# Building the relative-bias table in the first mixer's opening, and loading expert weights in 16 KB pieces

## The reference

```python
def clamped_swiglu(hgu):
    gate, up = jnp.split(hgu, 2, axis=-1)
    gate = jnp.minimum(gate, SWIGLU_LIMIT)
    up = jnp.clip(up, -SWIGLU_LIMIT, SWIGLU_LIMIT)
    return gate * jax.nn.sigmoid(SWIGLU_ALPHA * gate) * (up + 1)
...
        return clamped_swiglu(xb @ w1[e] + b1[e]) @ w2[e] + b2[e]
```

```python
        bias = rel_bias[t5_bucket(sel - tq[None, :, None])]
        logits = logits + jnp.moveaxis(bias, -1, 2).astype(jnp.float32)
```

## Time and profile before

| | |
|---|---|
| median of 3 runs | 2480.67 us (2477.57 to 2481.11) |
| the profiled execution, its own time | 2479.01 us |
| its span | 2476.8 us |
| TensorE (matmuls) busy | 2194.0 us, 89% |
| VectorE busy | 841.2 us, 34% |
| ScalarE busy | 352.9 us, 14% |
| transfers | 603.43 MB, mean 244 GB/s |
| granted TensorE clock, mean | 0.96 |

### The profile page before, as it was taken

The page is one execution under the profiler, slowest core; times in us unless marked ns, Lnnn a source line. Parts: engine busy times, 40 slices in busy tenths (PEclk is TensorE's granted clock), DMA queues, the critical chain, the costliest instruction groups (busy, mean ns, idle before and its releaser), DMA issues.

```text
span 2476.8 us, 23637 instructions
## 1 busy us (share of the span) xinstructions
PE 2194.0 (89%) x9258; PEld 1129.7 (46%) x9259; DVE 841.2 (34%) x1276; ACT 352.9 (14%) x740; POOL 44.4 (2%) x25
## 2 busy tenths in 40 slices
PE   4998877899999988999998599988999899898999
PEld 2856632222222222222222264445884554547873
DVE  1454431222222222222221234532561066414650
ACT  1123110000000000000001112211110122202110
POOL 0001100000000000000000001000000010000000
PEclk9998978999999999999999799999999999899999
DMA  9464038999999999999999534223442533133441
GB/s 364 144 244 163 28 78 300 409 410 410 410 410 410 410 410 410 410 410 410 410 410 409 213 135 170 92 94 105 150 156 86 177 132 126 68 102 126 146 158 46
DMA packets 219517, 603.43 MB, mean 244 GB/s; under 512 B 10159, under 2 KB 66495, under 8 KB 219315
## 3 DMA queue, kind: packets, MB, share of 16 engines
q1 hardware_dynamic: 219442, 602.42, 64.6%
HBM read 599.25 MB, written 3.15 MB: 243 GB/s over the span
## 4 chain that ended last, share of the span: by engine, by line
issue 59%; PE 35%; DVE 3%; ACT 1%; DMA 1%; POOL 1%; SPq 0%; DVEq 0%; POOLq 0%
PE bank L560 16%; PE bank L568 7%; PE bank L2002 6%; PE bank L767 2%; PE bank L2233 1%; PE bank L552 1%; DMA ring<-in_w_ada_dram 1%; POOL arena L1518 0%; PE bank L434 0%; PE bank L421 0%; PE bank L1909 0%; DVE hbuf L1647 0%; DVE arena L1648 0%; DVE normw L2118 0%; DVE arena L2090 0%
## 5 line engine op out<-in xcount | busy, mean ns | idle before, releaser
L1193 PE MATMUL bank<-ring,arena 128*64 128x512 f32 x3168 | 719.1, 601 | 103.2 <-DMA ring<-in_w_dram 101.9
L1193 PEld LDWEIGHTS bank<-ring,arena 128*64 128x64 f32 x3168 | 217.7, 138 | 595.4 <-issue 410.4
L560 PE MATMUL bank<-hTbuf,ring 128*128 128x256 f32 x1856 | 401.8, 379 | 4.4 <-ACT hTbuf L1755 3.6
L560 PEld LDWEIGHTS bank<-hTbuf,ring 128*128 128x128 f32 x1856 | 352.4, 190 | 53.0 <-issue 5.5
L2002 PE MATMUL bank<-ring 128*128 128x512 f32 x352 | 151.4, 592 | 0.0
L568 PE MATMUL bank<-ring,hTbuf 128*128 128x512 f32 (+2 forms) x384 | 151.2, 554 | 0.0
L992 DVE COPY arena<-bank 128x256 f32<-128x256 f32 x33 | 14.0, 424 | 370.2 <-PE bank L1187 370.2
L1717 DVE SCALAR_TENSOR_TENSOR arena<-bank,arena 128x254 f32<-128x254 f32 (+1 forms) x176 | 76.6, 477 | 127.7 <-ACT arena L1848 126.1
L1919 PE MATMUL bank<-ring,hTbuf 128*128 128x512 f32 x256 | 115.3, 604 | 0.0
L978 DVE RECIPROCAL arena<-arena 128x512 f32<-128x512 f32 x33 | 110.6, 3353 | 1.1
L568 PEld LDWEIGHTS bank<-ring,hTbuf 128*128 128x128 f32 x384 | 72.7, 190 | 75.1 <-issue 71.8
(11 more groups left out here) (348 smaller groups left out, 1697.5 us busy)
## 6 DMA issues: line engine op xcount, KB each, us to landing
ring<-in_w_dram SPq DMA_DIRECT2D x198, 2048.0 KB, 23.7
ring<-in_w_up_dram SPq DMA_DIRECT2D x44, 1024.0 KB, 6.4
ring<-in_w_in_dram SPq DMA_DIRECT2D x21, 2048.0 KB, 8.3
ring<-in_w_ada_dram SPq DMA_DIRECT2D x12, 2048.0 KB, 8.0
ring<-in_w_down_dram SPq DMA_DIRECT2D x10, 2048.0 KB, 7.8
ring<-in_w_out_dram SPq DMA_DIRECT2D x6, 2048.0 KB, 9.1
ring<-in_w_in_dram SPq DMA_DIRECT2D x4, 1024.0 KB, 14.0
ring<-in_w_proj_a_dram SPq DMA_DIRECT2D x2, 2048.0 KB, 7.9
```

The lines of the kernel that those rows point to most:

```text
L560: ins = pe.matmul(B.bank(name, j)[:, i * T:(i + 1) * T], w[:, k, (first + i) * P:(first + i + 1) * P], hT[:, k, :], start=(k == 0), stop=( ...
L1193: ins = pe.matmul(bank[g * SLOTS:(g + 1) * SLOTS, :], lhsT, rhs[:, g * CH:(g + 1) * CH], start=start, stop=stop)
```

## The change

The bias table's product moves to TensorE's opening, behind the transpose of the convolution's weights; ScalarE instead of VectorE scales it into `relrow`, which now lies at `12 * D + 512`. SyncE writes the row as it is (16 KB) to a new tensor `bias_row` ahead of load 12, and expands it from device memory to device memory behind load 21. The expert chunks are cut differently: chunk 0 to 3 is now a block of 256 rows with gate and up columns, each partition takes two neighbouring rows (16 KB in one piece), and a `w2` chunk gives each partition four neighbouring rows. `up` adds for each chunk to both banks, so that gate and up are both complete with chunk 3. So that the features match these rows, the second modulation deals the features out anew (`dealt`, `held`), the router's weights are loaded in the same order, and the product L988 reads with a step of four.

```diff
-    for name, n in (("ag0", 1), ("ad0", 4), ("hT", 4), ("convT", 1), ("qk", 4), ("dq", 6), ("v", 2), ("z", 2), ("ab", 1),
+    for name, n in (("ag0", 1), ("ad0", 4), ("hT", 4), ("convT", 1), ("rel", 1), ("qk", 4), ("dq", 6), ("v", 2), ("z", 2), ("ab", 1),
...
+        def dealt(row):
+
+            return [row[:, 2 * P * c:2 * P * (c + 1)].rearrange("p (q k) -> p k q", k=2) for c in range(4)]
+
+        def held(row):
+            return [split(row[:, 2 * P * c:2 * P * (c + 1)], 2) for c in range(4)]
...
-                then(v.scalar_tensor_tensor(out=h[:, tt, :], in0=x[:, tt, :], scalar=rs[:, tt:tt + 1], in1=scale,
-                                            op0=ALU.mult, op1=ALU.mult))
+                for hp, xp, sp_ in zip(held(h[:, tt, :]), deal(x[:, tt, :]), deal(scale)):
+                    ins = v.scalar_tensor_tensor(out=hp, in0=xp, scalar=rs[:, tt:tt + 1], in1=sp_, op0=ALU.mult, op1=ALU.mult)
+                then(ins)
...
-            modulate(v, then, 1, 1, ("ad2", 3), 2)
+            modulate(v, then, 1, 1, ("ad2", 3), 2, dealt, held)
...
-            v.wait_ge(*B.ready("rel"))
-            v.tensor_scalar(relrow, B.bank("rel")[0:8, :], float(AHD ** 0.5), None, ALU.mult).then_inc(B.free("rel"), 1)
...
-            v.scalar_tensor_tensor(out=act_b, in0=ub, scalar=1.0, in1=gb_, op0=ALU.add, op1=ALU.mult).then_inc(F["act"], 1)
+            v.scalar_tensor_tensor(out=act_b.rearrange("p (q a) -> p q a", q=4), in0=ub.rearrange("p (a q) -> p q a", q=4),
+                                   scalar=1.0, in1=gb_.rearrange("p (a q) -> p q a", q=4),
+                                   op0=ALU.add, op1=ALU.mult).then_inc(F["act"], 1)
...
-                for ch, (bank, flag) in enumerate(((GB, "gate_h"), (GB, "gate_f"), (UB, "up_h"), (UB, "up_f"))):
+                for ch in range(4):
                     w, landed = wts(i, ch)
                     pe.wait_ge(*landed)
-                    for k in range(4):
-                        ins = halves(bank, xe[:, 4 * (ch % 2) + k, :], w[:, k, :], False, ch % 2 == 1 and k == 3)
-                    ins.then_inc(F[flag], 1)
+                    for m, bank in enumerate((GB, UB)):
+                        for k in range(2):
+                            ins = halves(bank, xe[:, 2 * ch + k, :], w[:, k, m * D:(m + 1) * D], False, ch == 3 and k == 1)
+                        if ch == 3:
+                            ins.then_inc(F[("gate_f", "up_f")[m]], 1)
+                    if ch < 3:
+                        ins.then_inc(F[f"c{ch}"], 1)
...
-            rows = slice((ch % 2) * CH, (ch % 2 + 1) * CH)
             if ch < 4:
-                src = A["w1"][0, e, rows, (ch // 2) * D:(ch // 2 + 1) * D]
-            else:
-                src = A["w2"][0, e, rows, :]
-            return src.rearrange("(k p) n -> p k n", p=P)
+                return A["w1"][0, e, 2 * P * ch:2 * P * (ch + 1), :].rearrange("(p k) n -> p (k n)", p=P)
+            return A["w2"][0, e, CH * (ch - 4):CH * (ch - 3), :].rearrange("(p k) n -> p (k n)", p=P)
...
-            sp.wait_ge(*B.taken("rel"))
-            sp.dma_start(scratch.rearrange("p h n -> h p n"), relrow.unsqueeze(1).to_broadcast([8, P, REL]))\
-              .then_inc(S["rel_out"], 16)
...
-                                       (wrt, A["w_router"][0].rearrange("(k p) n -> p k n", p=P)),
+                                       (wrt.rearrange("p (c k) n -> p c (k n)", c=4),
+                                        A["w_router"][0].rearrange("(c p k) n -> p c (k n)", c=4, p=P)),
...
+                if n == ada_at[1]:
+
+                    sp.wait_ge(*B.taken("rel"))
+                    sp.dma_start(row8, relrow).then_inc(S["rel_row"], 16)
...
+            sp.wait_ge(S["rel_row"], 16)
+            sp.dma_start(scratch.rearrange("p h n -> p (h n)"), row8.rearrange("h n -> (h n)").partition_broadcast(P))\
+              .then_inc(S["rel_out"], 16)
...
+            act.wait_ge(*B.ready("rel"))
+            act.activation(relrow, B.bank("rel")[0:8, :], ACT.Copy, scale=float(AHD ** 0.5)).then_inc(B.free("rel"), 1)
...
+            pe.wait_ge(*B.room("rel"))
+            pe.matmul(B.bank("rel")[0:8, :], thin[0:32, 0:8], c("bucket", 32), start=True, stop=True)\
+              .then_inc(B.full("rel"), 1)
```

More of the change, by code:

```diff
@@ L237 @@
     "ov_hot",
-    "rel_out", "rel_in",
+    "rel_row", "rel_out", "rel_in",
     "b12_in", "norm_in",
@@ L246 @@
     "pgt_f", "pgt",
-    "gate_h", "gate_f", "up_h", "up_f", "y_h",
+    "c0", "c1", "c2", "gate_f", "up_f", "y_h",
     "g_in", "gu_out",
@@ L392, in bview, with whole, modulate @@
             return b[:].rearrange("p (a b) -> p a b", a=n)
-        def modulate(v, then, sh, nw, job, count):
+        def dealt(row):
+            return [row[:, 2 * P * c:2 * P * (c + 1)].rearrange("p (q k) -> p k q", k=2) for c in range(4)]
+        def held(row):
+            return [split(row[:, 2 * P * c:2 * P * (c + 1)], 2) for c in range(4)]
+        def whole(row):
+            return [row]
+        def modulate(v, then, sh, nw, job, count, deal=whole, held=whole):
             shift, scale = mod[:, 3 * sh * D:(3 * sh + 1) * D], mod[:, (3 * sh + 1) * D:(3 * sh + 2) * D]
@@ L400, in modulate @@
             for tt in range(TT):
-                then(v.scalar_tensor_tensor(out=h[:, tt, :], in0=x[:, tt, :], scalar=rs[:, tt:tt + 1], in1=scale,
-                                            op0=ALU.mult, op1=ALU.mult))
+                for hp, xp, sp_ in zip(held(h[:, tt, :]), deal(x[:, tt, :]), deal(scale)):
+                    ins = v.scalar_tensor_tensor(out=hp, in0=xp, scalar=rs[:, tt:tt + 1], in1=sp_, op0=ALU.mult, op1=ALU.mult)
+                then(ins)
             for tt in range(TT):
-                v.tensor_tensor(h[:, tt, :], h[:, tt, :], shift, ALU.add).then_inc(S["h_new"], 1)
+                for hp, sp_ in zip(held(h[:, tt, :]), deal(shift)):
+                    ins = v.tensor_tensor(hp, hp, sp_, ALU.add)
+                ins.then_inc(S["h_new"], 1)
         def head(place):
@@ L868, in build_program @@
         r3T = split(area(11 * D, 4 * P), 4)
-        relrow = area(11 * D + 512, REL)[0:8, :]
+        relrow = area(12 * D + 512, REL)[0:8, :]
         xe = split(area(0, CH), KT)
@@ L1140, in moe_t, with view @@
             ins.then_inc(B.full("gT"), 1)
-            pe.wait_ge(*B.room("rel"))
-            pe.matmul(B.bank("rel")[0:8, :], thin[0:32, 0:8], c("bucket", 32), start=True, stop=True)\
-              .then_inc(B.full("rel"), 1)
             wait_all(pe)
-            def view(s):
-                return slot(s).rearrange("p (k n) -> p k n", k=4)
+            def view(s, ch):
+                return split(slot(s), 2 if ch < 4 else 4)
             def weights(i, ch):
@@ L1152, in weights @@
                     s = (N1 + ch) % RING
-                    return view(s), (slot_in[s], 16 * (per_slot[s] + 1))
+                    return view(s, ch), (slot_in[s], 16 * (per_slot[s] + 1))
                 if ch < 4:
                     s = (N1 + 4 + ch) % RING
-                    return view(s), (slot_in[s], 16 * (per_slot[s] + (1 if ch < 2 else 2)) + 16 * (i - 1))
+                    return view(s, ch), (slot_in[s], 16 * (per_slot[s] + (1 if ch < 2 else 2)) + 16 * (i - 1))
                 if isinstance(i, int) and i == NE - 1:
                     s = (N1 + ch) % RING
-                    return view(s), (slot_in[s], 16 * (per_slot[s] + NE))
+                    return view(s, ch), (slot_in[s], 16 * (per_slot[s] + NE))
                 s = (N1 + 4 + ch) % RING
-                return view(s), (slot_in[s], 16 * (per_slot[s] + 2) + 16 * i)
+                return view(s, ch), (slot_in[s], 16 * (per_slot[s] + 2) + 16 * i)
             def over_weights(j, ch):
                 s = (N1 + ch) % RING
-                return view(s), (over_in[s], 16 + 16 * j)
+                return view(s, ch), (over_in[s], 16 + 16 * j)
             def gather(F, n):
@@ L1319, in later_sync @@
                     sp.dma_start(split(biasbuf[:, at:at + 4 * nk], 4), src).then_inc(S["rel_in"], 16)
-            ups, downs = ["gate_h", "gate_f", "up_h", "up_f"], ["y_h", "y_f"]
+            ups, downs = ["c0", "c1", "c2", "up_f"], ["y_h", "y_f"]
             def fetch(s, e, ch, landed):
-                sp.dma_start(slot(s).rearrange("p (k n) -> p k n", k=4), expert_chunk(e, ch)).then_inc(landed[s], 16)
+                sp.dma_start(slot(s), expert_chunk(e, ch)).then_inc(landed[s], 16)
             for ch in (2, 3):
@@ L1342, in later_sync @@
             nov = sp.value_load(ovi[0:1, 15:16], min_val=0, max_val=NOV)
-            before = [("up_h", NE), ("up_f", NE), ("y_h", NE - 1), ("y_f", NE - 1), ("y_h", NE), ("y_f", NE)]
+            before = [("c2", NE), ("up_f", NE), ("y_h", NE - 1), ("y_f", NE - 1), ("y_h", NE), ("y_f", NE)]
             with sp.Fori(0, NOV) as j:
```

5 lines of the change are left out of this document (3 added, 2 removed).

## The result

The changed kernel takes 2421.14 us (median of 4 runs, 2411.08 to 2422.56), beside 2479.12 us (4 runs, 2473.81 to 2481.11) for the kernel before. The ratio is 0.9744, 95% interval 0.9715 to 0.9774: faster by 2.6%. The two medians by themselves are 58.0 us apart, a quotient of 0.9766, which lies in that interval too. The forecast of 2412 is 9.1 us (0.4%) too low; the measured time lies inside its whole range, 2400 to 2453, and just above the narrower 2404 to 2421. The profiled execution is the fastest of the four: 2411.08 us around a span of 2409.2, where the sum gave 2412.2.

A forecast was written before the change was run, and what follows sets the result against it. The expert weight stream was taken as the bound; -71.3 us from earlier start and larger pieces plus 4.5 us took 2479.01 to 2412.2, said as 2412. Its own range was 2404 to 2421, the whole range 2400 to 2453.

The forecast's parts named there:

- What bounds the kernel: Expert stage: weight transfers at 409 to 410 GB/s set the pace; TensorE needs 90.8% of the time.
- the rival in which TensorE becomes the bound: Expert loop: with 1.5 us of slack a round, late chunks cost TensorE time; 2428 us, chance 0.08.
- The wait that goes: SyncE's 43.5 us wait for the bias table's expansion goes; first fetch near 355.1, start alone worth -32.3 us.
- The piece size: Expert chunks in 16 KB instead of 4 KB pieces: 4.91 us a chunk instead of 5.127.
- pieces that stay as dear: Rival: expert stream stays at 410 GB/s, only the earlier start counts; 2451 us, chance 0.14.
- a bad pitch: Rival: 16 KB pieces on a 16 KB pitch stream slower, 5.42 us a chunk; 2503 us, chance 0.07.
- the ceiling of 4.83 us: Rival: no fixed part per piece, 4.83 us a chunk, 14 us less; 2398 us, chance 0.03.
- First landing and last: Expert stream: expert 2's first chunk lands at 388.7, the last awaited at 1267.6 instead of 1338.95, -71.3 us.
- Gate and up by chunk: Both banks complete only with the fourth chunk: hidden in the loop, +4.2 us once in the overflow block.
- The small ones: Opening product +0.6, second modulation +1.0, routing's end -1.9 us: together -0.3 us.
- The sum of 2412.2 us: Whole kernel: -71.3 + 4.5 = -66.8 us from the profiled execution's 2479.01 us.

The follow-up runs named there:

- table-alone kernel: Kernel before with only the bias table moved, expert chunks still in 4 KB pieces: 2447.1 us, ratio 0.9877.
- the kernel with the old form at the new place: Changed kernel with the bias table's expansion again straight from eight partitions in 2 KB pieces, at the new early place: 2419.94 us (one run).
- the 8 KB kernel: Changed kernel with expert chunks in 8 KB pieces, and the plain second modulation and old router weight order: 2427.22 us, ratio 0.978.
- the two repeats: Changed kernel unaltered, measured twice more beside other kernels: 2418.67 us, ratio 0.9744, and 2416.49 us, ratio 0.9741.
- the two with the overflow block by bank: Changed kernel with only the overflow block's up products ordered gate bank first, then up bank, measured twice: 2406.52 us, ratio 0.9731, and 2410.49, ratio 0.9724.

## Why the prediction was right, step by step

**What bounds the kernel.** Held. The weights set the pace to the end of the stage, TensorE waits 34.5 us in 830 us, so it works 95.8% of a round of 29.4 us: 28.1, where the step had 27.9. The margin is 1.2 us and not 1.5, still enough: the rival in which TensorE becomes the bound didn't come. It is near, though; another 4% on the stream would find TensorE there.

**The wait that goes.** Held: no wait, the first fetch at 356.75 (forecast 355.1), no idle at expert 1. The table-alone kernel had its last awaited chunk at 1305.28 against a computed 1306.6. That the expansion has cover was shown by the kernel with the old form at the new place: there it slowed the prefetch by some 20 us, and the closing product was no later.

**The piece size.** Held, and it is the step that decided. Forecast 4.91 us a chunk from a line through 2 KB and 4 KB, which a burst of 13.4 KB bore out; measured 4.90, with the 8 KB kernel on the same line. The rivals that went with it are excluded: pieces that stay as dear would have left 410 GB/s, a bad pitch less, and the ceiling of 4.83 us isn't reached because 9 ns a piece do remain.

**First landing and last.** 1267.6 forecast, 1266.86 measured. That it is so near is partly luck: in the five profiled executions whose program is the same up to this point (this one, the two repeats, the two with the overflow block by bank) it came at 1263.00 to 1268.11.

**Gate and up by chunk.** In the loop hidden, as the step said: there is no wait for VectorE's chain between two experts. In the overflow block the idle is 6.17 us, forecast 5.86 with 0.3 for the strided product beside it: 6.16. That product takes 1.06 us instead of 0.69, both its inputs read in steps of four.

**The small ones.** Of their sum of -0.3 us, -0.07 is left where it counts: expert 1's products begin at 376.19, before at 376.26. But the way there isn't the forecast's. Rows of the changed kernel:

```profile
51.65 1.02 PE L2208 MATMUL bank<-con,small 32*8 32x512 f32 x2
```

```profile
312.49 3.38 DVE L413 SCALAR_TENSOR_TENSOR hbuf<-x,small,arena 128x256 f32<-128x256 f32 x8 [0.67 <-POOL small L2077]
315.91 2.77 DVE L417 TENSOR_TENSOR hbuf<-hbuf,arena 128x256 f32<-128x256 f32 x8
```

```profile
323.33 7.01 PE L1118 MATMUL bank<-arena,hTbuf 128*128 128x32 f32 x32 [0.92 <-ACT hTbuf L557]
```

And the last of them in the kernel before:

```profile
325.79 4.82 PE L1104 MATMUL bank<-arena,hTbuf 128*128 128x32 f32 x32 [0.89 <-ACT hTbuf L543]
```

The opening's extra product took 1.02 us here, and from the transposes (L566) to the first projection it takes 4.68 us, before 4.67: nothing lost. In five of the other nine profiled executions with this product it took 1.87 us, and in three of them, which have this opening unchanged, that stretch is 5.67 to 5.68 us, 1.0 lost. The forecast's 0.6 is the middle of two cases that each occur. The modulation takes 3.38 + 2.77 us instead of 2.60 + 2.36: +1.2, forecast +1.0. It begins 3.7 us earlier than before, at 312.49, for which the sum had no term; in the two repeats it begins at 314.01 and 317.68, so this is the spread of executions and not the change. The router's products then take 7.01 us instead of 4.82, with a granted clock of 0.50 from 324 to 332 us where it was 0.71. The pick begins 0.44 us behind the start of the copy ahead of it instead of 2.30, the -1.9 of the forecast; in time it is 341.17 instead of 343.31. And expert 0's 64 products took 15.96 us instead of 13.95, at 0.87 from 352 to 364 us instead of 1.00. The total came out by terms that cancelled, and that was luck.

**The sum and the median.** The sum of 2412.2 us was for an execution like the profiled one, and such an execution took 2411.08; that the two profiled executions spent the same time in the second block (1078.0 and 1077.9 us) was luck too, as the repeat with 10.2 us more there shows. What was mis-sized is the last step, from there to the median: it set the execution against three runs that lay within 3.5 us and moved it by nothing. Over more runs the kernel before spreads from 2468 to 2491 us, and the changed one from 2409 to 2423. In the one pair of traces taken apart nearly all of it lies in the second block, at a lower granted clock; that it does so in every run isn't shown, nor what sets the clock. A median of four can come out 10 us off for that, as here. The ratio of 0.9744 is 64 us of 2479, with 56 to 71 as its interval, and both the forecast's 66.8 and the medians' 58.0 lie in it. The narrower range of 2404 to 2421 had no term for this spread, and the median, 2421.14, fell just outside.

## What to carry to other kernels

Where a stream of weights sets the pace, fit time per piece against piece size from whatever sizes the trace already has; here the stream's own 4 KB and a short burst of 2 KB gave the pace at 16 KB to 0.2%, and a burst of 13.4 KB bore the line out beforehand. Look in the queue of the engine that issues transfers for one wait that is not for a buffer, and move what it waits for ahead of a long quiet stretch: if it fits in there, its own speed doesn't matter. Compare a forecast with the spread of several executions before calling a small term confirmed. When computation is reordered to suit a transfer, look for the one pass that has no neighbour to hide its tail; it can keep the old order alone.

## What the runs showed of the hardware

- In a stream at a saturated queue, pieces of 4, 8 and 16 KB went at 410, 422 and 428 GB/s. Worked out from these three, each of 16 engines spends 9 ns per piece and 151 ns per 4 KB; an estimate from the slope alone would be 435 GB/s (16 x 4096 B / 150.6 ns).
- 2 MB written to device memory from eight partitions, in 2 KB pieces, went at some 49 GB/s and took 44 us; the same 2 MB read from and written to device memory were through in a few us, in slices of 350 to 437 GB/s.
- In one opening with idles of 3.05 and 4.93 us TensorE's granted clock was 0.50 for the work that followed, and eight products took 5.61 us instead of 3.70.
- Two executions of one program differed by 11.6 us. Of these 10.2 lay behind the first block, where two windows of 100 us had a granted clock of 0.88 and 0.89 instead of 0.95.
- VectorE's product over 512 elements took 1.06 us with both inputs read in steps of four, and 0.69 us with plain inputs.
